# Moving the RWKV columns down by one row: one copy of 127 partitions, or two of 112 and 15

## What is computed

```
cols_a, cols_b, gate_a, gate_b = split_cols(h @ w_in[l], IN_SIZES)
def token_shift(t):
    return jnp.pad(t[:, :-1], ((0, 0), (1, 0), (0, 0)))
...
cols = cols + (token_shift(cols) - cols) * mu
r, k, v, wd, ad, gd = split_cols(cols, RWKV_SIZES)
```

## Time and profile before

| | |
|---|---|
| runs | 3659.84, 3670.2, 3673.36 us; median 3670.2 us |
| profiled execution, first to last instruction (its span) | 3652.9 us |
| what lies around the span | the profiled execution's time over all is not listed; the three runs are 6.9 to 20.5 us longer than the span |
| TensorE busy | 3174.9 us, 87% of the span |
| VectorE, ScalarE, GpSimd busy | 1574.6, 1042.0, 106.8 us |
| mean granted TensorE clock | 0.923 of full speed |
| VectorE idle before L1641 (twice) | 160.3 us |

### The profile page before, as it was taken

How to read it: one execution, slowest core, us unless ns; L and a number is a source line. 1 busy time by engine, 2 the same in 40 slices (tenths; PEclk the granted TensorE clock), 3 DMA queues, 4 the chain that set the end, 5 groups by cost and what they waited for, 6 DMA issues and landing times.

```text
span 3652.9 us, 33457 instructions
## 1 busy us (share of the span) xinstructions
PE 3174.9 (87%) x14288; PEld 2376.9 (65%) x14288; DVE 1574.6 (43%) x1875; ACT 1042.0 (29%) x1220; POOL 106.8 (3%) x85
## 2 busy tenths in 40 slices
PE   8977999877899899781989799963988899999999
PEld 6864768766765688440774487531854688888887
DVE  4455244533552344351742454244622544444444
ACT  4333134332341243030110343121011343343433
POOL 0010000000110000000000000000000000000000
PEclk9988999988889999895899899986899899999999
DMA  7440445456434344421104254511013355555554
GB/s 259 162 151 24 150 138 185 150 164 177 138 118 147 127 171 152 154 92 52 46 24 151 69 184 144 184 65 54 16 58 111 114 175 189 182 175 185 175 187 144
DMA packets 249045, 487.97 MB, mean 134 GB/s; under 512 B 36258, under 2 KB 67618, under 8 KB 248514
## 3 DMA queue, kind: packets, MB, share of 16 engines
q1 hardware_dynamic: 248576, 482.17, 39.5%
q10 hardware_dynamic: 320, 3.66, 0.3%
HBM read 481.08 MB, written 4.69 MB: 133 GB/s over the span
## 4 chain that ended last, share of the span: by engine, by line
PE 76%; DVE 9%; DMA 4%; another core or an unknown queue 4%; ACT 2%; SPq 2%; POOL 1%; issue 1%; DVEq 0%; POOLq 0%; ACTq 0%
PE psum L352 18%; PE psum L349 15%; PE psum L351 15%; PE psum L350 15%; PE psum L1860 2%; SPq L291 2%; PE psum L1936 2%; PE psum L688 2%; PE psum L663 2%; PE psum L467 2%; PE psum L1847 1%; DMA weight_ring<-in_ffn_w_gate 1%; DMA weight_ring<-in_moe_wd 1%; ACT weight_high_halves L338 1%
## 5 line engine op out<-in xcount | busy, mean ns | idle before, releaser
L344 DVE TENSOR_TENSOR weight_ring_low_halves<-weight_ring,weight_high_halves 128x2048 fp32r<-128x2048 f32 (+1 forms) x346 | 743.2, 2156 | 954.3 <-ACT weight_high_halves L338 954.3
L349 PE MATMUL psum<-weight_high_halves,stage_area_halves 128*128 128x512 f32 (+2 forms) x2616 | 1009.8, 386 | 53.2 <-DVE weight_ring_low_halves L344 48.3
L351 PE MATMUL psum<-weight_high_halves,stage_area_halves 128*128 128x512 f32 (+2 forms) x2616 | 1000.8, 383 | 0.0
L350 PE MATMUL psum<-weight_ring_low_halves,stage_area_halves 128*128 128x512 f32 (+2 forms) x2616 | 1000.0, 382 | 0.0
L338 ACT ACTIVATE weight_high_halves<-weight_ring 128x2048 fp32r<-128x2048 f32 (+1 forms) x346 | 622.6, 1806 | 853.9 <-PE psum L351 397.6
L352 PE MATMUL psum<-weight_ring,stage_area 128*128 128x512 f32 (+2 forms) x1600 | 672.8, 581 | 11.6 <-DMA weight_ring<-in_w_in 6.5
L349 PEld LDWEIGHTS psum<-weight_high_halves,stage_area_halves 128*128 128x128 f32 x2616 | 498.9, 191 | 150.8 <-DVE weight_ring_low_halves L344 47.1
L351 PEld LDWEIGHTS psum<-weight_high_halves,stage_area_halves 128*128 128x128 f32 x2616 | 497.7, 190 | 98.5
L350 PEld LDWEIGHTS psum<-weight_ring_low_halves,stage_area_halves 128*128 128x128 f32 x2616 | 497.7, 190 | 93.7
L352 PEld LDWEIGHTS psum<-weight_ring,stage_area 128*128 128x128 f32 x1600 | 305.0, 193 | 365.9 <-issue 364.1
L448 ACT ACTIVATE stage_area<-psum 128x512 f32<-128x512 f32 (+2 forms) x126 | 71.8, 579 | 657.4 <-PE psum L352 393.0
(11 more groups left out here) (244 smaller groups left out, 2316.4 us busy)
## 6 DMA issues: line engine op xcount, KB each, us to landing
weight_ring<-in_ffn_w_down SPq DMA_DIRECT2D x44, 1024.0 KB, 4.9
weight_ring<-in_ffn_w_gate SPq DMA_DIRECT2D x40, 1024.0 KB, 5.2
weight_ring<-in_ffn_w_up SPq DMA_DIRECT2D x40, 1024.0 KB, 5.1
weight_ring<-in_moe_wd SPq DMA_DIRECT2D x40, 1024.0 KB, 4.9
weight_ring<-in_w_in SPq DMA_DIRECT2D x36, 1024.0 KB, 5.2
weight_ring<-in_moe_wg SPq DMA_DIRECT2D x32, 1024.0 KB, 5.3
weight_ring<-in_moe_wu SPq DMA_DIRECT2D x32, 1024.0 KB, 5.2
weight_ring<-in_mem_w_kv SPq DMA_DIRECT2D x16, 1024.0 KB, 5.1
```

Source lines behind the costliest of these rows:

```text
L344: v.raw.tensor_tensor(self.low_half(name), self.in_slot(name), self.high_half(name), ALU.subtract).then_inc(*v.mark("low_halves", ("halves ...
L349: pe.raw.matmul(out, a[1], w[0], start=start, stop=False)
L350: pe.raw.matmul(out, a[0], w[1], start=False, stop=False)
L351: return pe.raw.matmul(out, a[0], w[0], start=False, stop=stop)
```

## The change

The copy of rows 0 to 126 of `colsA` to rows 1 to 127 of `colsS` becomes two copies: rows 0 to 111 to rows 1 to 112, and rows 112 to 126 to rows 113 to 127. They are issued one after the other from ScalarE's queue, and the copy of the single row for half 1 stays behind them. All three still count on `rows_shifted`, so the mix waits for 48 in place of 32 in each layer.

```
     def shift_scalar(self, act, l):
         A, B = self.colsA, self.colsS
-        act.raw.dma_start(B[1:P, :, :], A[0:P - 1, :, :]).then_inc(*act.mark("rows_shifted", ("shift", l, 0), by=16))
+        act.raw.dma_start(B[1:113, :, :], A[0:112, :, :]).then_inc(*act.mark("rows_shifted", ("shift", l, 0), by=16))
+        act.raw.dma_start(B[113:P, :, :], A[112:P - 1, :, :]).then_inc(*act.mark("rows_shifted", ("shift", l, 2), by=16))
         act.raw.dma_start(B[0:1, 1, :], A[P - 1:P, 0, :]).then_inc(*act.mark("rows_shifted", ("shift", l, 1), by=16))
```

## The result

The changed kernel took 3524.45 us in the median of four runs (3515.35 to 3534.49), the kernel before 3665.02 us in four (3658.48 to 3673.36). The ratio of the runs is given as 0.9624, with a 95% interval of 0.9601 to 0.9647: faster by 3.8%. At a base of 3665 us that is 137.8 us, with an interval of 129 to 146 us; the two medians themselves lie 140.6 us apart.

A forecast was written before the change was run, and what follows sets the result against it. The prediction took the 127-row shift copy, on one DMA engine, as the bound in that stage. Gains of 72.3 and 71.9 us, 144.1 in sum, from the 3670.2 us median gave 3526 us, range 3508 to 3546.

The forecast's parts named there:

- The bound: At the shift in each layer, the 127-row copy bounds: 80.27 and 79.85 us from issue to mix.
- an unknown queue: Queue the profile can't name, here ScalarE's own; 78.01 us of the layer 0 wait chain before the mix.
- One engine of sixteen: The 127-row copy sits on one DMA engine, share 0.06, 27 GB/s; 112 and 15 rows get 16 and 15 engines.
- The time of the new copies: Shift in each layer, first issue to mix: 8.0 us, between bounds of 6.6 and 11.1 us.
- The doubled bound: Upper bound of the new copies per layer: moving time doubled for SBUF to SBUF, 2.1 + 9.0 = 11.1 us.
- The base: Whole kernel: 144.1 us taken from the median of 3670.2 us; runs lie 6.9 to 20.5 us above the profiled span.
- What is late next: At layer 0's mix, TensorE, ScalarE and SyncE have 8 us to spare, so all of the 72 us is gained.
- its stall of 39 us: ScalarE's second copy issue in layer 1 took 39.00 us; the prediction costed its return at nothing.
- The clock: TensorE restarts after the shift at the lower level, 0.50, as before; costed at 0 with 4.3 us either way.
- The 15 rows on one engine: Rival at the shift: only multiples of 16 are spread; 7.4 us more per layer, 3541 us; chance 0.09.
- the split does nothing: Rival at the shift: 112 rows stay on one engine or copies run in turn; 3670 to 3674 us; chance 0.05.
- sixteen engines hold each other up: Rival at the shift: slower than before if all engines together move under 20 GB/s; 3714 us at 18; chance 0.02.

The follow-up runs named there:

- 113 and 31 rows: First copies of two kernels like the changed one but cut elsewhere: 113 and 14 rows, 3650.6 us; 96 and 31 rows, 3569.78 us.
- second profile: The changed kernel profiled once more, nothing altered; 10.2 and 10.7 us from first issue to mix.
- 113 and 14 rows: The changed kernel with its two copies cut at 113 and 14 rows in place of 112 and 15; 3650.6 us, ratio 0.9961 to the kernel before.
- early 127-row copy: The kernel before with its one copy issued before the attention ends, the shifted columns having their own place, and the memset at the layer's start; 3582.2 us.
- the 31 rows: The changed kernel with its two copies cut at 96 and 31 rows in place of 112 and 15; 3569.78 us in one run.
- 126 rows: The changed kernel with its two copies cut at 126 rows and 1 row in place of 112 and 15; 3530.2 us, ratio 0.9633 to the kernel before.

## Why the prediction was right

**The bound.** Right. The group with 7.8 us of work and 160.3 us of idle time, the chain through "an unknown queue" and the lists that all stood still said that the copy was the bound, and the whole of what was taken off it came off the end.

**One engine of sixteen.** Right, and shown from both sides: 113 and 31 rows stay on one engine, 112, 15, 126 and 96 don't, and the packets count 1, 1, 16, 15, 14 and 16 engines. The share of 0.06 in the earlier trace rows was the telling number, and 27 GB/s per engine holds (27.8 from 13 rows fewer).

**The time of the new copies.** The mechanism was right, the size too small. I summed 8.0 us per layer with 11.1 as the upper bound; it is 10.5 and 11.9, and 10.2 and 10.7 in the second profile. Three parts of the term were off. Sixteen engines that copy from SBUF to SBUF moved 258 to 301 GB/s together in single microseconds between 1650 and 1655 us, 16 to 19 each, not 27 each; 1.83 MB at 280 GB/s are 6.5 us and not 4.5. The two small copies land one after the other: in layer 0 the three land 8.4, 9.5 and 10.5 us after the first issue, in layer 1 8.4, 9.4 and 11.8, where I gave the two 0.8 us together. The doubled bound had seen the first and not the second, and layer 1's 11.9 lies above it. The half row that I put on the fullest engine is spread over all sixteen, 448 bytes each; that is small, 0.3 us the other way. The gain was 137.8 us in the two stretches, not 144.1.

**The base.** The 3526 us are nearer to the 3524.45 than the sum deserves. I took 144.1 us from the first median, 3670.2; with the fourth run the kernel before stands at 3665.0, 5.2 us lower. Between the medians the gain is 140.6 us, 3.5 less than I summed. The two errors go against each other and leave 1.7 us, which is luck. I also put the runs 6.9 to 20.5 us above the span. A run is 1.8 us longer than its own span (3532.46 against 3530.7); the profiled execution of before was simply shorter than the others.

**What is late next.** Right: TensorE, ScalarE and SyncE were through before the columns were mixed, and no stall came back on ScalarE (issues of 0.6 to 2.2 us). That its stall of 39 us was tied to a long list on one engine is borne out by 113 and 14 rows and by the early 127-row copy, which have it, and by all kernels with shorter lists, the 31 rows among them, whose issues took at most 2.2 us each. Why only some of the issues behind a long list stall (in layer 0 of the kernel before none did) stays open.

**The clock.** Right that the restart would be at the lower level, 0.50 at 1664 to 1669 us and on to 1677.2. What followed cost 4.5 + 0.3 = 4.8 us in the two layers (35.0 in place of 30.5 us, 37.7 against 37.4), and 5.4 + 0.0 in the second profile: a little more than the 4.3 that I gave for both. It can't be put down to TensorE's shorter idle time: with 113 and 14 rows, where that is nearly as long as before, the stretch of layer 0 took 35.9 us too, and with 126 rows 31.8. Of the 35.0 us 20 are at the lower level, of the 30.5 us 9. Why the one or the other comes isn't settled by the runs. The lag of 9.1 us ahead of the first shift had no term in the sum at all.

**The rivals.** The 15 rows on one engine: fallen, there is no tail. That the split does nothing: fallen; the advice of the Trainium skill, page "DMA: Bandwidth & Descriptors", section "Rules for kernel authors", against two transfers to disjoint partition halves doesn't carry to a transfer whose row count keeps it on one engine. That sixteen engines hold each other up: true by a third, 280 GB/s in place of 16 x 27 = 432, and far from the 20 GB/s from which it would have decided.

**Left open.** Why 126 and 1 rows take 9.3 and 10.1 us, 0.6 to 1.8 less than 112 and 15 (each in one or two profiles), although the fullest engine has 9 rows and not 8; and why the large copy takes 2 us longer to land behind the small ones.

## What to carry to other kernels

Look at the DMA share while a copy is waited for: 0.06 is one engine of sixteen, and a row count with no divisor from 2 to 16 (127, 113, 31) does that. Cut such a copy into counts that divide well. Then ask why it is waited for at all: another 1% lay in buffers that forced the copy, the row vectors and `mu` to wait for the attention or the mix. The list in which a copy is issued counts too: the work behind it in that list waits for the issue.

## What the runs showed that was not expected

- Issuing a DMA can block the engine that issues it: 39.00, 33.88, 31.41 and 30.21 us on ScalarE, each time behind a copy with over 100 rows on one engine, though not behind every such copy.
- A copy of one row isn't confined to one engine: the half row left 16 packets of 448 bytes.
- SBUF to SBUF on all engines ran at 258 to 301 GB/s in layer 0, a load from HBM at 391.
- A shorter idle time of TensorE paid twice. When the wait for the row vectors fell away (5.59 to 1.13 us of idle time), the clock stayed up as well and the next 20 matmuls took 3.5 us in place of 6.8.
